# Stick-breaking attention: the low parts of the next pair's q and k move from GpSimd to VectorE, in two steps, and the value differences and their transposes come two steps later

## The reference, cut to what matters

```python
def stick_breaking_mix(q, k, v):          # (B, T, H, d), T = 1024, H = 8, d = 64
    scale = d ** -0.5
    for blk in range(T // SB_BLOCK):      # blocks of 128 query tokens
        t0, t1 = blk * SB_BLOCK, (blk + 1) * SB_BLOCK
        z = einsum('bthd,bshd->bhts', q[:, t0:t1], k[:, :t1]) * scale
        causal = arange(t1)[None, :] < arange(t0, t1)[:, None]
        log_1mb = where(causal, -softplus(z), 0.0)
        rem = cumsum(log_1mb, axis=3, reverse=True) - log_1mb
        a = where(causal, exp(log_sigmoid(z) + rem), 0.0)
        out = einsum('bhts,bshd->bthd', a, v[:, :t1])
```

## Time and profile before

| what | value |
|---|---|
| median of three runs | 3175.54 us (3169.97 to 3178.27) |
| the profiled execution's own time | 3176.49 us |
| its span in the profile | 3174.9 us |
| mean granted clock of TensorE | 0.964 of full speed |
| TensorE (PE) busy | 2996.1 us, 94% of the span |
| VectorE (DVE) busy | 1572.5 us, 50% |
| ScalarE (ACT) busy | 1018.1 us, 32% |
| GpSimd (POOL) busy | 117.2 us, 4% |

### The profile page before, as it was taken

How to read it: one execution, slowest core, us unless ns; L and a number is a source line. 1 busy time by engine, 2 the same in 40 slices (tenths; PEclk the granted TensorE clock), 3 DMA queues, 4 the chain that set the end, 5 groups by cost and what they waited for, 6 DMA issues and landing times.

```text
span 3174.9 us, 35161 instructions
## 1 busy us (share of the span) xinstructions
PE 2996.1 (94%) x14780; PEld 2498.6 (79%) x14780; DVE 1572.5 (50%) x1986; ACT 1018.1 (32%) x1377; POOL 117.2 (4%) x66
## 2 busy tenths in 40 slices
PE   8999989997999999999999977899999999999998
PEld 6888878886788888887778856788878888888877
DVE  4256766524443443345642277577435454445454
ACT  3143445433211111112431166676322211212131
POOL 0011211022000000000100000000000000000000
PEclk9999989998999999999999978998999999999999
DMA  4101220032111111111121100000211111111122
GB/s 159 54 27 54 82 86 1 27 101 92 60 47 49 52 40 53 54 47 40 47 86 60 34 14 9 21 1 1 100 34 53 47 47 54 47 54 47 49 77 80
DMA packets 45805, 165.59 MB, mean 52 GB/s; under 512 B 5424, under 2 KB 5936, under 8 KB 45648
## 3 DMA queue, kind: packets, MB, share of 16 engines
q1 hardware_dynamic: 45648, 163.34, 15.7%
HBM read 142.09 MB, written 21.23 MB: 51 GB/s over the span
## 4 chain that ended last, share of the span: by engine, by line
PE 87%; DVE 7%; ACT 3%; issue 2%; DMA 0%; SPq 0%; ACTq 0%; DVEq 0%
PE PS L274 22%; PE PS L276 22%; PE PS L278 22%; PE PS L476 2%; PE PS L477 2%; PE PS L478 2%; PE PS L1184 2%; PE PS L699 2%; PE PS L2654 1%; PE PS L1154 1%; PE PS L1169 1%; PE PS L2208 1%; PE PS L2176 1%; DVE w_lo L268 1%; PE PS L2645 1%
## 5 line engine op out<-in xcount | busy, mean ns | idle before, releaser
L274 PE MATMUL PS<-u_hi_f,w_hi 128*128 128x512 f32 x1408 | 440.9, 395 | 27.2 <-DVE u_lo_f L395 15.1
L276 PE MATMUL PS<-u_lo_f,w_hi 128*128 128x512 f32 x1408 | 437.6, 392 | 0.0
L278 PE MATMUL PS<-u_hi_f,w_lo 128*128 128x512 f32 x1408 | 437.5, 392 | 0.0
L268 DVE TENSOR_TENSOR w_lo<-w_raw,w_hi 128x1024 fp32r<-128x1024 f32 x215 | 267.8, 1254 | 290.9 <-ACT w_hi L262 290.9
L262 ACT ACTIVATE w_hi<-w_raw 128x1024 fp32r<-128x1024 f32 x215 | 225.6, 1052 | 572.5 <-PE PS L278 431.8
L274 PEld LDWEIGHTS PS<-u_hi_f,w_hi 128*128 128x128 f32 x1408 | 266.7, 190 | 87.2 <-DVE w_lo L268 13.9
L276 PEld LDWEIGHTS PS<-u_lo_f,w_hi 128*128 128x128 f32 x1408 | 267.4, 190 | 56.4
L278 PEld LDWEIGHTS PS<-u_hi_f,w_lo 128*128 128x128 f32 x1408 | 266.8, 190 | 56.0
L274 PE MATMUL PS<-f_ah,w_hi 128*128 128x512 f32 x704 | 218.5, 392 | 10.3 <-DVE f_al L1687 10.3
L276 PE MATMUL PS<-f_al,w_hi 128*128 128x512 f32 x704 | 218.1, 391 | 0.0
L278 PE MATMUL PS<-f_ah,w_lo 128*128 128x512 f32 x704 | 217.9, 391 | 0.0
(11 more groups left out here) (381 smaller groups left out, 4980.1 us busy)
## 6 DMA issues: line engine op xcount, KB each, us to landing
w_raw<-in_weights SPq DMA_DIRECT2D x217, 512.0 KB, 3.6
H<-in_x_t SPq DMA_DIRECT2D x16, 512.0 KB, 4.4
stick_kept<-stick_stage SPq DMA_DIRECT2D x12, 512.0 KB, 2.9
mixer<-stick_kept SPq DMA_DIRECT2D x9, 512.0 KB, 6.9
p_kept<-p_stage SPq DMA_DIRECT2D x8, 512.0 KB, 4.0
h_kept<-H SPq DMA_DIRECT2D x8, 512.0 KB, 5.7
H<-h_kept SPq DMA_DIRECT2D x8, 512.0 KB, 7.2
p_pp<-p_kept SPq DMA_DIRECT2D x8, 512.0 KB, 6.4
```

Source lines behind the costliest of these rows:

```text
L268: dve.tensor_tensor(self.w_lo[i][:], self.w_raw[i][:], self.w_hi[i][:].bitcast(F32), ALU.subtract).then_inc(*self.s("w_lo").up(g))
L274: ins = e.matmul(banks[i], lh, rh[i], start=first, stop=False)
L276: ins = e.matmul(banks[i], lh, rl[i], start=False, stop=False)
L278: ins = e.matmul(banks[i], ll, rh[i], start=False, stop=last)
```

## The change

GpSimd's part (`pool_stick_parts`, `pool_stick_prepare`, `pool_stick` and its call) is gone. VectorE forms `ql` in step 7 and `kl` in step 8, the differences in step 9. TensorE turns the halves in steps 10 and 11, ScalarE copies them out in steps 10 and 11. ScalarE's high parts stay in steps 5 and 6.

```diff
     def pe_stick_prepare(self, pair):
 
         pe, steps = self.nc.tensor, self.stick_raw(pair)[0]
-        for _ in range(8 if pair else 0):
+        for _ in range(10 if pair else 0):
             yield
...
     def dve_stick_prepare(self, pair):
         dve = self.nc.vector
         q, k, v = self.stick_raw(pair)
-        for _ in range(8 if pair else 0):
+        if pair:
+            qh, ql, kh, kl = self.sb_parts[pair % 2]
+            for _ in range(7):
+                yield
+            dve.wait_ge(*self.s("sb_hi").at(pair))
+            dve.tensor_tensor(ql[:], q, qh[:].bitcast(F32), ALU.subtract)
+            yield
+            dve.tensor_tensor(kl[:], k, kh[:].bitcast(F32), ALU.subtract).then_inc(*self.s("sb_parts").up(pair))
             yield
         dve.wait_ge(*self.stick_parts(pair))
...
             act.activation(kh[:], k, ACT.Copy).then_inc(*self.s("sb_hi").up(pair))
-            yield
-            yield
+            for _ in range(4):
+                yield
...
-    def pool_stick_prepare(self, pair):
-        for _ in range(7):
-            yield
-        self.pool_stick_parts(pair)
-        yield
...
     def pool_program(self):
         self.pool_hgrn()
-        self.pool_stick()
         self.pool_out1()
```

More of the change, by code:

```diff
@@ L1049, in stick_parts @@
         return self.s("sb_parts").at(pair) if pair else self.s("sb_parts_first").at()
[L1051 to L1057, removed]
     def sides(self, parts, steps):
@@ L1241, in act_stick_square @@
                        accum_out=self.sb_sums[:, t, pair:pair + 1]).then_inc(*self.s("sb_squares").up(n))
[L1243 to L1248, removed]
     def dve_stick(self):
```

## The result

The changed kernel takes 3152.27 us, the median of four runs (3148.63 to 3152.58), against 3175.68 us before. The ratio is 0.9926, 95% interval 0.9914 to 0.9938: 0.7% less, 23.4 us. A later comparison with the same kernel gave 3151.13 us (3144.01 to 3154.59) against 3175.56, ratio 0.9922 (0.9910 to 0.9935). The forecast was 3150.2 us. The profiled execution went from 3176.49 to 3152.44 us, 24.0 us less (forecast 25.3).

A forecast was written before the change was run, and what follows sets the result against it. TensorE's waits around three preparations and the slow clock behind them were taken as the bound, 28.1 us at most. Savings of 9.0 + 6.4 + 9.9 = 25.3 us took the median from 3175.54 to 3150.2 us, range 3143 to 3161 us.

The forecast's parts named there:

- What bounds the kernel: TensorE around the three preparations: its waits and the slow clock behind them, 28.1 us at most to win.
- Why VectorE was late: Differences needed in step 8 stood behind chunk 7's scan; GpSimd's subtractions held up scans, 4.2 and twice 2.0 us.
- Added subtractions at 1.2 us: Six low-part subtractions moved to VectorE, taken at 1.2 us each, bounds nothing and 2.5 us.
- Second and third preparation: TensorE waits 0.2 us at the turning in each; 6.4 and 9.9 us saved, slow clock included.
- First preparation: The 2.92 us row-copy wait goes, TensorE waits 2.4 us at the turning; 9.0 us saved.
- the signs that I had named: Among them: one TensorE wait of 2 to 3 us for the differences in the first preparation, none above 0.5 in others.
- Scans that don't shrink: Rival: something other than GpSimd lengthens VectorE's scans; only 4.6 us saved, 3171 us; chance 0.05.
- VectorE as the pacer: Rival: added passes delay scans 7 and 8, TensorE waits at its transposes, clock stays low; 3195 us; chance 0.02.
- The clock falling at the wait that remains: Rival: the clock falls behind the first preparation's 2.4 us wait, costing 2.3 to 5.8 us; 3152.5 to 3156 us; chance 0.2.
- The high end: Low parts at 2.5 us each on VectorE: 17.5 us saved, 3158 us, 3161 us with the runs' spread.
- Sum: Savings over the three preparations, 9.0 + 6.4 + 9.9 = 25.3 us, expected to reach the end whole.

The follow-up runs named there:

- The move alone: Kernel before with differences in step 9 and turning in steps 10 and 11, GpSimd still forming the low parts; 3155.72 us, ratio 0.9950.
- the engine alone: Changed kernel with VectorE forming both low parts in step 7, differences back in step 8, turning in steps 8 and 9; 3168.07 us, ratio 0.9980.
- the gating moved: Changed kernel with VectorE's gating of the other mixer in steps 11 to 18 instead of 5 to 12; 3147.61 us, ratio to the kernel before 0.9915.
- idle subtractions: Changed kernel plus two unused GpSimd subtractions of 128x1024 on a spare tile in each preparation; 3159.34 us, one run.
- idle memsets: Changed kernel plus five unused GpSimd memsets of a spare tile in each preparation; 3152.89 us, one run.
- both parts in one step: Changed kernel with `kl` formed straight behind `ql` in step 7, all else in place; 3150.65 us against 3151.13 us for the changed kernel.
- waits filled: Kernel before with 36 idle TensorE transposes ahead of each wait for the differences; 3165.33 us, ratio 0.9971.

## Why the prediction was right

*What bounds the kernel.* Right. The last pair as a measure of undisturbed steps gave 28.1 us that could be won at most; the stretch became 24.5 us shorter.

*Why VectorE was late.* Right in both parts, and the runs give their weights. The move alone shortens the stretch by 18.5 us, the engine alone by 6.2, both together by 24.5. The order was the larger part: GpSimd's subtractions cost mostly through one place, the row copy in the first preparation, and there through the slow clock: the move alone has 2.92 us of waits and the changed kernel 3.12, but the move alone has 13.7 us at 1.2 GHz and the changed kernel none.

*Added subtractions at 1.2 us.* 1.22 and 1.20 us.

*Second and third preparation.* The third gave 10.1 us (forecast 9.9). In both, the wait at the turning, forecast at 0.2 us, is nil, but with next to no margin: in the second the differences end at 509.10 us and the turning starts at 509.15. The second gave 5.2 instead of 6.4 us: its first steps now contain the wait of 1.13 us that ends at 478.21 us. That is the one term of the sum that was mis-sized, and the gating is why: VectorE worked off its backlog in steps 10 to 12, and I had followed it only to the turning.

*First preparation.* 9.2 us saved (forecast 9.0), with a wait of 1.99 us where 2.4 were forecast, but at another instruction. I had it at the turning, behind the differences. It sits one place earlier, at the product of chunk 6, which opens a new row and so needs the row copy that VectorE makes behind the scans of chunk 8. The copy ended at 469.56 us, the product began at 469.70 us. The length was close since differences and row copy lie 1.2 us apart on VectorE, with that product between them on TensorE; the calculation had not looked at that place, so the good number is in part luck. Of the signs that I had named, this one did not come: the wait that is left is not for the differences, and a second one is above the 0.5 us that I allowed.

*The wait of 1.13 us.* The profile names ScalarE's copy of chunk 9, which ended at about the same time. The code waits there for chunk 8's copy, long done, and for a row copy by VectorE. With the gating moved it goes, and the product starts before that copy of ScalarE's. So it was VectorE's.

*The rivals.* Scans that don't shrink: excluded by the changed kernel's own scans and by the idle subtractions and memsets. VectorE as the pacer: no wait at the transposes of the scans but one of 0.64 us at 457.57 us, which the kernel before has as well. The clock falling at the wait that remains: in neither of the changed kernel's two profiles, but in the profile of the variant with both parts in one step, where it lengthened the way between the turnings by 1.5 us, less than the 2.3 us at which I had its lower end, and the stretch by 0.2.

*The high end.* It was not put to the test, since the low parts took 1.2 us and not 2.5. But its working was at odds with the rows: it saved 17.5 us with waits of 5.0 and twice 2.8 us at full clock, where the rows had the clock fall behind 2.9 us.

*Sum.* 24.0 us by the profiled executions and 23.4 and 24.4 us by the two comparisons of medians, against 25.3.

## What to carry to other kernels

When an engine waits for a preparation, compare the step in which it asks with the steps that the supplier has ahead of it: asking two steps later cost nothing here and was worth more than speeding up the supplier. VectorE's two-input work and GpSimd subtractions should not stand at the same time, and even a copy of two columns on VectorE can be held up until they end; GpSimd memsets did no such harm here. And in a stream that is else dense, price a stop of TensorE with the slow clock behind it, which here added 12.5 us to 15.6 us of standing, and take that price as a range.

## What was not expected of the hardware

The price of the slow clock is not a property of the wait. The times at 1.2 GHz below are added up from windows of 1 us; a fall can lie within the wait. Of the time at 1.2 GHz in which TensorE worked, about half was lost: 5.8 of 12.5 us in the third preparation before.

| kernel | waits, us | us at 1.2 GHz |
|---|---|---|
| before, first preparation | 2.92, then 4.06 | 13.7 over both |
| before, second and third | 4.33; 4.32 | 6.8; 13.7 |
| move alone | 2.92 | 13.7 |
| waits filled, first preparation | 2.92 | 6.8 |
| engine alone | 5.27; 4.00; 4.00 | 6.8; 10.2; 6.8 |
| idle subtractions | 2.00; 1.53; 1.47; 1.47 | 3.4; 3.4; 3.4; none |
| idle memsets | 2.14 | none |
| both low parts in one step | 1.98 | 3.4 |
| changed kernel, both profiles | 1.99 | none |

Waits of 1.5 to 2.1 us were followed by nothing or by 3.4 us, waits of 2.9 us and more by 6.8 to 13.7 us. What decides between them is not shown by these runs. And idle work in place of the waits, which left VectorE as late as before, made the kernel 10.2 us faster, as expected for that run.
